# State-space products of two steps in one burst, and the MLP loop written out

## The reference

```python
x = x + jnp.square(jax.nn.relu(h @ w_mlp_up[l])) @ w_mlp_down[l]
```

```python
bu = jnp.einsum('bsgh,gph->bsgp', uf.astype(jnp.complex64), b_bar)
_, states = lax.associative_scan(combine, (a_el, bu), axis=1)
y = jnp.einsum('bsgp,ghp->bsgh', states, c_mat).real + d.astype(f32) * uf
y = jax.nn.gelu(y.reshape(bsz, seq, BRANCH_W)).astype(u.dtype)
```

## Time and profile before

| | us |
|---|---|
| median of 3 runs (2452.26 to 2454.85) | 2452.55 |
| the profiled execution | 2454.28 |
| its span in the profile | 2452.5 |
| PE busy in it | 2429.2 |

### The profile page before, as it was taken

One profiled execution on the slowest core, in us unless ns is written; L12 is line 12 of the kernel. 1 busy time (PEld: TensorE's weight loads), 2 busy tenths in 40 slices (PEclk: granted clock), 3 DMA queues, 4 the chain that ended last, 5 costly groups with the idle time before them and its releaser, 6 DMA issues.

```text
span 2452.5 us, 31953 instructions
## 1 busy us (share of the span) xinstructions
PE 2429.2 (99%) x13482; PEld 1996.0 (81%) x13482; DVE 1534.6 (63%) x1530; ACT 1030.0 (42%) x860; POOL 274.8 (11%) x226
## 2 busy tenths in 40 slices
PE   8999999999999999999999999999999999999998
PEld 7888888878888888888888888887777778888886
DVE  6465556557676455445445567789999955446564
ACT  4553345334344443443443434443433444544332
POOL 1002201210000000000000000054556400000000
PEclk9999999999999999999999999999999999999999
DMA  6343354346755455555555555665555576566753
GB/s 257 135 164 115 136 184 168 108 149 245 262 193 184 177 189 190 188 189 191 186 191 194 187 196 205 224 242 192 189 187 194 187 284 234 173 240 227 257 197 137
DMA packets 84220, 475.10 MB, mean 194 GB/s; under 512 B 8704, under 2 KB 8832, under 8 KB 32512
## 3 DMA queue, kind: packets, MB, share of 16 engines
q1 hardware_dynamic: 84096, 473.32, 54.2%
HBM read 450.21 MB, written 23.07 MB: 193 GB/s over the span
## 4 chain that ended last, share of the span: by engine, by line
PE 96%; DMA 1%; DVE 1%; ACT 1%; issue 0%; SPq 0%; DVEq 0%; ACTq 0%
PE acc L2098 29%; PE acc L2100 29%; PE acc L2099 29%; PE banks L2262 3%; PE banks L2111 2%; PE banks L2318 1%; DMA raw<-in_w 1%; PE banks L2385 1%; PE banks L2398 1%; DVE w_lo L1272 0%; ACT w_hi L820 0%; DMA av<-spilled 0%; DVE stats L1324 0%; PE banks L2438 0%; PE banks L2420 0%; PE banks L2236 0%
## 5 line engine op out<-in xcount | busy, mean ns | idle before, releaser
L1272 DVE TENSOR_TENSOR w_lo<-raw,w_hi 128x2048 fp32r<-128x2048 f32 x394 | 908.1, 2308 | 552.7 <-ACT w_hi L820 551.5
L820 ACT ACTIVATE w_hi<-raw 128x2048 fp32r<-128x2048 f32 x394 | 751.8, 1914 | 591.0 <-DMA raw<-in_w 588.8
L2098 PE MATMUL acc<-w_hi,a_hi 128*128 128x512 f32 x2112 | 840.5, 398 | 5.8 <-DVE a_lo L1308 3.1
L2099 PE MATMUL acc<-w_lo,a_hi 128*128 128x512 f32 x2112 | 824.7, 390 | 0.0
L2100 PE MATMUL acc<-w_hi,a_lo 128*128 128x512 f32 x2112 | 824.4, 390 | 0.0
L2098 PEld LDWEIGHTS acc<-w_hi,a_hi 128*128 128x128 f32 x2112 | 397.3, 188 | 104.2 <-issue 15.3
L2100 PEld LDWEIGHTS acc<-w_hi,a_lo 128*128 128x128 f32 x2112 | 397.4, 188 | 84.9
L2099 PEld LDWEIGHTS acc<-w_lo,a_hi 128*128 128x128 f32 x2112 | 397.8, 188 | 78.5
L2098 PE MATMUL acc<-w_hi,b_hi 128*128 128x512 f32 x928 | 364.2, 392 | 0.0
L2100 PE MATMUL acc<-w_hi,b_lo 128*128 128x512 f32 x928 | 361.5, 390 | 0.0
L2099 PE MATMUL acc<-w_lo,b_hi 128*128 128x512 f32 x928 | 361.2, 389 | 0.0
(11 more groups left out here) (356 smaller groups left out, 1642.4 us busy)
## 6 DMA issues: line engine op xcount, KB each, us to landing
raw<-in_w SPq DMA_DIRECT2D x395, 1024.0 KB, 4.8
spilled<-stage SPq DMA_DIRECT2D x72, 256.0 KB, 6.0
gate_in<-spilled SPq DMA_DIRECT2D x20, 512.0 KB, 5.8
x_rows<-in_x SPq DMA_DIRECT2D x4, 512.0 KB, 8.2
x_rows<-in_x SPq DMA_DIRECT2D x1, 2048.0 KB, 9.2
mem_rows<-in_mem SPq DMA_DIRECT2D x2, 1024.0 KB, 5.8
spilled<-stage_b SPq DMA_DIRECT2D x8, 256.0 KB, 5.9
out<-y_rows SPq DMA_DIRECT2D x3, 512.0 KB, 2.7
```

Source lines behind the costliest of these rows:

```text
L820: act.activation(w_hi[:, n % HIGH, :], raw[:, n % RAW, :], ACT.Copy)\
L1272: dve.tensor_tensor(w_lo[:, n % RAW, :], raw[:, n % RAW, :], w_hi[:, n % HIGH, :].bitcast(F32), ALU.subtract).then_inc(lo_split, 1)
L2098: pe.matmul(o, hi[:, tk], wh, start=first, stop=False)
L2099: pe.matmul(o, hi[:, tk], wl, start=False, stop=False)
```

## The change

Four things change together.

1. PE makes the state products of two steps (i and i+1, i even) in one burst of 8 matmuls that uses all four row groups and writes all four banks. The output products of two steps (i-2 and i-1) are also one burst of 8, in all four column groups of bank 2. Odd steps have no PE part.
2. Banks 2 and 3 hold the products of the odd step. ACT copies them to a new SBUF buffer `bu_odd` right after the burst, and DVE's four multiplications of odd steps read `bu_odd` in place of the banks.
3. A step's parts stand at places 0, 2, 4, 6 of its seven (before: 0, 2, 3, 5). The gelu moves from part 3 of the even step to part 1 of the odd step after it. `s_out` gets a third buffer, `s_third`.
4. The MLP loop is written out: all 394 units are straight code, waits are against constants, and waits that were left out inside the loop are written for every piece.

```diff
-        for part, place in enumerate((0, 2, 3, 5)):
+        for part, place in enumerate((0, 2, 4, 6)):
             put_at(2 * (a + 3) + 1 + SSM_PLACES * i + place, "ssm", i, part)
...
+        s_third = region("s_third", 40, [P, 2, 2, T])
+        bu_odd = at("bu_odd", bb + 28 * KB, [P, 2, NW])
+        s_buf = lambda i: s_third if i % 3 == 2 else s_out[:, i % 3]
...
-        def drive(me, slot_work, after_loop):
...
+        def drive(slot_work):
+            for n in range(UNITS):
                 slot_work(n)
...
# ACT
             def ssm(i, part):
-                if part == 3 and i >= 2 and i % 2 == 0:
-                    ct = (i - 2) // 2
-                    act.wait_ge(dve_done, me.at(f"ssm{i}.ysum"))
+                if i < 16 and i % 2 == 0 and part == 0:
+                    act.wait_ge(pe_done, me.at(f"ssm{i}.bu"))
+                    act.wait_ge(dve_done, me.at(f"ssm{i - 1}.turned" if i else "ssm0.turned"))
+                    for g in range(2):
+                        act.activation(bu_odd[:, g], bank(2 + g), ACT.Copy).then_inc(act_done, me.done(f"ssm{i + 1}.taken"))
+                if (part == 1 and i >= 3 and i % 2) or (part == 3 and i == 16):
+                    ct = (i - 2) // 2 if i == 16 else (i - 3) // 2
+                    act.wait_ge(dve_done, me.at(f"ssm{2 * ct + 2}.ysum"))
                     act.activation(uT[:, ct, :], prod_y(ct), ACT.Gelu_apprx_tanh)\
                         .then_inc(act_done, me.done(f"gelu{ct}"))
...
# DVE
-                    bu = [banks[:, 0:2, z * T:(z + 1) * T] for z in range(2)]
+                    bu = [(bu_odd if k else banks[:, 0:2])[:, :, z * T:(z + 1) * T] for z in range(2)]
...
-                    dve.wait_ge(pe_done, me.at(f"ssm{i}.bu"))
+                    if k:
+                        dve.wait_ge(act_done, me.at(f"ssm{i}.taken"))
+                    else:
+                        dve.wait_ge(pe_done, me.at(f"ssm{i}.bu"))
...
-                    if i >= 2:
-                        dve.wait_ge(pe_done, me.at(f"ssm{i - 1}.y"))
+                    if i >= 3:
+                        dve.wait_ge(pe_done, me.at(f"ssm{(i - 3) // 2 * 2 + 2}.y"))
...
# PE
-                    b = [this_bank(g, f"bu{i}", g, f"ssm{i}.turned") for g in range(2)]
+                    b = [this_bank(q, f"bu{i}", q, f"ssm{i}.turned" if q < 2 else f"ssm{i + 1}.taken") for q in range(4)]
                     for z in range(2):
-                        for g in range(2):
-                            rs = slice(64 * (i % 2) + 32 * g, 64 * (i % 2) + 32 * g + 32)
-                            ins = pe.matmul(b[g][:, z * T:(z + 1) * T], b_in[rs, ct, z, :], uT[rs, ct, :],
-                                            start=True, stop=True)
+                        for q in range(4):
+                            ins = pe.matmul(b[q][:, z * T:(z + 1) * T], b_in[32 * q:32 * q + 32, ct, z, :],
+                                            uT[32 * q:32 * q + 32, ct, :], start=True, stop=True)
...
+                if i and part == 1:
+                    pe.wait_ge(dve_done, me.at(f"ssm{i - 1}.s", "ssm.c_out"))
+                    b = this_bank(2, f"ssy{ct - 1}", 0, f"ssm{i}.ysum")
                     for z in range(2):
-                        for g in range(2):
...
+                        for q in range(4):
+                            j = i - 2 + q // 2
+                            ins = pe.matmul(b[32 * q:32 * q + 32, 0:T], c_out[:, z, 2 * j + q % 2, :],
+                                            s_buf(j)[:, z, q % 2, :], start=z == 0, stop=z == 1)
```

More of the change, by code:

```diff
@@ L232, in schedule @@
     put(end(f"w_mlp_down{p}", 2) - 2, "load_g_final")
-    put(end("w_mlp_up", 2 * p), "hidden", p, 0)
-    put(end("w_mlp_up", 2 * p + 1), "hidden", p, 1)
+    for p in range(1, NPIECE):
+        put(end("w_mlp_up", 2 * p), "hidden", p, 0)
+        put(end("w_mlp_up", 2 * p + 1), "hidden", p, 1)
     put(end("xa_wv", 1) + 2, "ssm_small", 0)
@@ L781, in _ @@
             ends = {FIRST[i + 1] - 1: i for i in SPILLS}
-            n = 0
-            while n < UNITS:
-                if n == LOOP0:
-                    with sp.Fori(0, LOOPS) as it:
-                        for m in range(LOOP_UNITS):
-                            weight(n + m + RAW, it)
-                    n += LOOPS * LOOP_UNITS
-                    run_steps(me, steps, 2 * n)
-                    run_steps(me, steps, 2 * n + 1)
-                    continue
+            for n in range(UNITS):
                 if n + RAW < UNITS:
@@ L797, in _ @@
                     run_steps(me, steps, 2 * n + 1)
-                n += 1
-                if n != LOOP0 and n not in ends:
-                    run_steps(me, steps, 2 * n)
-                    run_steps(me, steps, 2 * n + 1)
+                if n + 1 not in ends:
+                    run_steps(me, steps, 2 * n + 2)
+                    run_steps(me, steps, 2 * n + 3)
             for t, n0, n1 in FINAL_DVE:
@@ L1257, in _ @@
             for n in range(UNITS):
-                if not LOOP0 <= n < LOOP0 + LOOP_UNITS:
-                    run_steps(me, steps, 2 * n)
-                    run_steps(me, steps, 2 * n + 1)
+                run_steps(me, steps, 2 * n)
+                run_steps(me, steps, 2 * n + 1)
         @block.vector
@@ L1833, in ssm @@
                 c_, s_ = rot[:, k, 0], rot[:, k, 1]
-                so = [s_out[:, k, z] for z in range(2)]
+                so = [s_buf(i)[:, z] for z in range(2)]
                 if i <= 15 and part == 0:
@@ L2069, in unit @@
                 if u == 0 and part == 0:
-                    if me.it is not None and n < LOOP0 + 8:
-                        pe.wait_ge(dve_emptied,
-                                   value(me, emptied(i - 2, "dve") - (NT if n == LOOP0 else 0), 8 * NT))
                     if i >= 2:
@@ L2374, in ssm @@
             def ssm(i, part):
-                if i <= 15 and part == 0:
-                    ct = i // 2
+                if i % 2:
+                    return
+                ct = i // 2
+                if i < 16 and part == 0:
                     pe.wait_ge(loaded["b_in"], 16)
```

104 lines of the change are left out of this document (23 added, 81 removed).

## The result

| | before | after |
|---|---|---|
| median of 8 runs (lowest to highest for after) | 2452.54 | 2460.94 (2458.68 to 2462.1) |
| the profiled execution | 2454.28 | 2461.05 |
| its span | 2452.5 | 2459.3 |

The changed kernel is slower: the ratio is 1.0032 with an interval of 1.0022 to 1.0042, 8.4 us. The forecast was 2455, its range 2442 to 2463, and the forecast's own narrower range was 2450 to 2460.

What follows compares the result with a forecast made beforehand. PE bounds the kernel before, DVE the changed state-space stage's inner pairs; 2454.28 + 0.4 (stage's pairs) + 2.4 (low clock) = 2457.1 us profiled, about 2455 median. Range 2442 to 2463, the forecast's own 2450 to 2460.

Steps and rivals of the forecast that it cites:

- PE's side: State-space stage: one burst of each kind per pair of steps saves PE 2.54 us, 43.17 to 40.63, 20.3 us over eight pairs.
- Rival 4: State-space bursts: four tiles run as two and two, PE's pair takes 42.7 us; +4, 2459 us; chance 0.06.
- DVE becomes the bound: State-space stage: DVE's pair is 35.2 us free plus 5.4 and 3.4 contention, 44.0; six pairs add 5.0 us.
- The odd half's 5.4 us of contention: Odd step on DVE: POOL's rotation loses all cover, eight small operations at 0.4 and two big at 1.1 us.
- Rival 1: State-space stage: PE stays the bound, contention not growing, all 20.3 us gained; 2432 us by the median; chance 0.07.
- The odd multiplications: Odd step on DVE: four multiplications reading `bu_odd` in SBUF run beside POOL at 1.1 us each, +1.7 us.
- Rival 2: Odd step: multiplications from SBUF don't suffer, or POOL slips behind the splits; pair 42.3, 2443 us; chance 0.20.
- PE's one wait per pair: State-space stage: PE waits once per pair for DVE's `w_lo`, losing about 3.4 us in one piece.
- The clock: Behind each new PE gap: granted clock falls, 0.4 us per pair (bounds 0 and 1.5), +2.4 for six.
- The last pair: End of the state-space stage: no rotation left for the odd half, DVE's work 38.6 us, below PE's: -2.5 us.
- The first pair: Start of the state-space stage: little POOL work, PE stays ahead: -2.5 us, 0.4 lost to new contention, -2.1.
- rival 3: State-space stage: `w_hi` late behind ACT's copies, DVE idle about 1.5 us per pair; +9.3, 2462 us; chance 0.22.

## Why the prediction came out as it did

*PE's side*: right, and shown alone by the runs without rotations: 2.52 us per pair against 2.54, four tiles at once in 1.12 us. Rival 4 is out.

*DVE becomes the bound*: right. The forecast pair of 44.0 us of DVE's work was measured as 44.11 where DVE never waits for `bu` (the run with the early copy), and its free part of 35.2 as 35.5. In the changed kernel itself it is 43.23, with 1.3 us of idle time. The odd half's 5.4 us of contention came out at 5.4: multiplications 1.7, the split 1.1, additions 0.9, scans 1.7. Rival 1 fell with this: it needed contention not to grow. The Trainium skill, TensorEngine Tiling, section PSUM Bottleneck, says that what empties PSUM may become the limit once TensorE is sped up. The runs agree that another engine than TensorE became the limit. But emptying PSUM isn't what limits here: read straight from PSUM, the products cost least.

*The odd multiplications*: right for this kernel. They take 1.105 us from `bu_odd` and 0.68 from the banks in the same kernel, and reading the banks was worth 15.8 us, of which 4.8 are the first pair's wait. Rival 2, that they don't suffer, is out for this kernel. With the parts at their old places they don't suffer (0.682 us), since DVE is there first, and yet that run is no faster. The prediction had each multiplication pay for the POOL operation beside it. What the runs show is that POOL's work has to be paid for somewhere, unless DVE reads PSUM beside it or is idle. The Trainium skill, GPSIMD Engine Reference, Key points, names instructions with two inputs in SBUF as those that contend. The 1.105 against 0.68 agrees, and so does the 8.42 us of a POOL operation that DVE held off. The split agrees too, by the price of 3.39 us that it pays if POOL is there first; the prediction had read it as an exception.

*PE's one wait per pair*: the place and the releaser are right. The size of 3.4 us holds nearly where the clock stays up: 44.38 - 41.24 = 3.1 us of PE's idle time in a pair of the run with the early copy, though in two gaps. In the changed kernel the gap is 1.95 us and another 1.9 is matmuls at the low clock (42.58 busy us for 40.65 us of work).

*The clock*: a low clock behind each gap was right for this run, and its price too high: 0.4 us per pair was put, and 0.15 is what pairs with it and without it differ by. Six pairs with all terms took +8.2 us over 6 x 43.17, where +5.0 for DVE and +2.4 for the clock had been put. That these come so close is in part luck. At full clock, in the run with the early copy, the six take +7.2, so DVE's term was 2.2 us too small, and the clock's, with 1.0 left for it, 1.4 too large.

*The last pair*: -2.52, put at -2.5.

*The first pair*: this is the step that failed most. The prediction gave it -2.1 us, and it was +2.24. It had the copies wait for PE's burst, "hidden, by half a microsecond", in every pair. In the first they wait for DVE, by a wait that stands in the diff, and the split behind them started 3.7 us behind the burst. The effect is that of rival 3, `w_hi` too late behind the copies, and beyond its point of decision (1.9 us). But it came in one pair and not in six, and by a wait for DVE that rival 3 doesn't name; it had put it down to a late burst and to the emptying of a chunk. The run with that wait moved gave 39.91 us for this pair, -2.0 against before, and so the term as forecast. That the time came out near rival 3's 2462 is therefore no support for rival 3.

In sum: the stage was put at +2.8 us and was +7.9. Of the 5.1 between them 4.3 are the first pair and 0.8 the other six. No change within 0.2% was held likeliest, with 0.44, and slower had 0.29; slower it is, by 0.32%. By the profile's 4.3 us the first pair alone would carry it over the 0.2%, but the medians don't bear that out: with that pair mended the kernel is still 6.4 us slower, ratio 1.0026. At 2460.94 the time lies just outside the forecast's own range of 2450 to 2460. The 1.6 us between what the medians differ by (8.4) and the profiles (6.8) is scatter that no run here resolves.

## What to carry to other kernels

Before work is taken from the busiest engine, add up the next one's work for the same stretch without its waits, with what a neighbour costs it when the waits are gone: here 2.8 us of slack were promised 2.5 us of use, and the reserve turned out to be the cover for POOL. A copy from PSUM to SBUF that frees a bank early moves the reader's operand to where it contends; it is worth its price only if the bank is needed. Moving such operations about in the queue didn't help here: what helped was to let the slower partner work while DVE reads PSUM. And when steps are widened to hold the slack, look for what stands behind them in the same order of places: a load that slipped past its reader cost 12 us here.

## What the runs showed of the hardware

- A DVE operation of 128x512 takes 0.68 us from PSUM and SBUF with POOL at work or without. With both inputs in SBUF it takes 1.105 if POOL's work had begun first, and 0.68 if POOL was being held off. POOL's small operation, 0.62 alone, takes 1.07 beside the former.
- Between a DVE split of 128x2048 and POOL the order of arrival counts: POOL's 0.62 becomes 2.60 if the split is there first, the split's 2.28 becomes 3.39 if POOL's 128x512 operation is. DVE can hold POOL off over several operations that follow each other without a pause: 8.42 us for a small one of POOL's, with the parts at their old places.
- Eight matmuls with 32 rows of contraction and 256 columns, in four row groups and four banks, take 1.12 us; four in two row groups took 1.06.
- A gap of 1.95 us on PE was followed by a granted clock of 0.66 in the changed kernel, and gaps of 2.71 us by none below 1.00 in the run with the early copy. The clock in the pair around it is 1.00. PE, at 1705.96 there:

```profile
1705.96 0.50 PE L2045 MATMUL acc<-w_hi,a_hi 128*128 128x512 f32 x1 [2.71 <-DVE w_lo L1223]
1706.29 0.40 PE L2046 MATMUL acc<-w_lo,a_hi 128*128 128x512 f32 x1
```

The length of the gap alone doesn't tell whether the clock falls. What else decides stays open.
